# A two-block model on one core: second output product issued inside the last head's work, and the end done by tiles of 128 tokens

## The chip, the core and the metric

The kernel runs on one NeuronCore of a Trainium2 chip. The engines named below are PE (TensorE, matrix products; PEld is its weight load), DVE (VectorE), ACT (ScalarE), POOL (GpSimd) and SP (SyncE, which here only issues DMAs). The metric is the device time of one execution in microseconds (us); lower is better. All data are float32, and each float32 product shows as two MATMUL records in the trace (a transposition by the identity as one).

## The reference

Two blocks on 512 tokens of width 1024. The first is a mixer and an MLP. The second is a latent attention and a gated recurrence of 8 heads, merged and multiplied by `w_out`, then a mixture of 32 experts, of which each token takes 4, and a last norm. What matters here:

```python
# second block, after the attention y_mla has been computed
y_hg = hgrn2_readout(o_forward + flip(o_backward), gate, hg_norm_g)      # 8 heads of 128 features
y    = sigmoid(p7) * y_mla + sigmoid(p8) * y_hg                          # merged, head by head
x    = x + mod[2] * (y @ w_out)                                          # second output product
h    = rmsnorm(x, norm_ffn_g) * (1 + mod[4]) + mod[3]
logits = h @ w_router + b_router                                         # top 4 of 32, softmax
out  = sum over k of prob[token, k] * y_rows[dest[token, k]]             # weighted sum of 4 expert rows
x    = x + mod[5] * out
return rmsnorm(x, final_norm_g)
```

## The kernel before

Activations lie with features on the partitions: `x` is 8 chunks (`DC`) of 128 features by 512 tokens (`T`). `TT` is 4 tiles of 128 tokens. Each engine has its own program, in one fixed order, and they meet at semaphores. Dense weights arrive through a ring of 5 SBUF slots, loaded by SP when the products of an older tile are done.

**The heads of the recurrence** (loop over `n` from L1069). A head is a chain through DVE, ACT, POOL and PE: gates, two scans, key transpositions (L1086), state terms (L1093), 14 levels of small products of 128 by 64 (L1109), a diagonal (L1111, L1112), the output sum (L1119 to L1121), a norm (`norm`, L884; the root on ACT L1326; `norm_spread`, L894), and `merge` on DVE (L1755 to L1759), which completes features 128n to 128n+127 of `ymla` and signals `s_hg`. PE fills its waits in head n with the input products of head n+1 (`Filler`, L847). Its share per place comes from `HEAD_SLOTS`. The last head, n = 7, has no filler.

**After the last head**: `products("out2")`, 64 products of 128x512 (L847) from `ymla` and four weight tiles, in pairs of banks which ACT copies to `mout2` (L1319). Then DVE adds 8 chunks to `x` (L1832), squares them one by one for the norm (L1572) while PE sums them (L884), and with root and reciprocal done writes the router input `h3` by two instructions a chunk (L1714, L1715). PE's 32 router products (L1136) wait for all 8 chunks. Then come transposition (L1144), top 4, the table of blocks, and the experts.

**The experts**: 84 fixed blocks of 32 token rows (L1206 up, L1228 down), their 12 tiles of 1 MB per expert streamed by SP through 20 slots (18 in `space`, two in `x`, whose content was stored to `x_kept`). Then comes a loop for rows left over, which turns once here, with 12 loads more (L726).

**The end**: the result rows of the loop are stored by ACT (L1515). When that has landed, POOL issues 16 indirect gathers of 128 rows (L809), four for each token tile, into 8 buffers. DVE weighs and sums four rows for each tile (L1989, L1992). PE transposes the sum (L1291), ACT copies it (L1550), and DVE scales it and adds it to `x` (L1977, L1978), which SP has loaded back after the last expert product (L728). Only when all four tiles are added do the squares, root, `norm_spread` and the 8 last products (L1580) run, each chunk of 128 features by 512 tokens followed by its store (L731).

## Time and profile before

| | |
|---|---|
| device time, median of 3 runs | 3423.99 us (3416.69 to 3424.7) |
| the profiled execution: its own time, its span | 3431.33 us, 3429.3 us |
| PE busy (matmul) | 3031.8 us, 88% of the span |
| DVE, ACT, POOL busy | 982.5, 650.8, 189.7 us |
| mean granted TensorE clock | 0.919 of 2.4 GHz |
| HBM read | 551.58 MB |
| chain that ended last | PE 76%, DMA 10%, DVE 9%, ACT 2% |

### The profile page before, as it was taken

How to read it: one execution, taken by the hardware profiler on the slowest of the kernel's cores; microseconds unless marked ns; L12 is line 12 of the kernel's file. 1: busy time of each engine (PE TensorE's matmuls, PEld its weight loads, DVE VectorE, ACT ScalarE, POOL GpSimd, SP SyncE). 2: the span in 40 equal slices, each digit the busy share in tenths (PEclk: the TensorE clock that was granted, in tenths of full speed). 3: DMA queues.
4: the chain of work that ended last, by engine and by line, in shares of the span. 5: the costliest groups of instructions: out<-in, count | busy, mean ns of one | idle time of the engine just before them, and what ended most of it. 6: DMA issues, size and time to landing. Idle time of an engine off the chain costs nothing.

```text
span 3429.3 us, 45858 instructions
## 1 busy us (share of the span) xinstructions
PE 3031.8 (88%) x19729; PEld 1567.8 (46%) x19729; DVE 982.5 (29%) x1996; ACT 650.8 (19%) x1345; POOL 189.7 (6%) x180
## 2 busy tenths in 40 slices
PE   6899879999798999899989967689999999999993
PEld 3554434444344666666656655343333333333331
DVE  2243130000313221554444553322121112121224
ACT  1133000000001333444344332110101101111100
POOL 0000000000000000111111111020000000000002
PEclk9998889999898999999999976789999999998996
DMA  4134212211200112311111010198999979999695
GB/s 155 46 144 174 84 49 74 76 59 63 90 30 25 39 44 78 143 44 44 43 44 40 22 37 2 75 409 337 416 374 381 416 309 416 401 392 384 263 378 224
DMA packets 116909, 585.12 MB, mean 171 GB/s; under 512 B 10244, under 2 KB 21540, under 8 KB 69860
## 3 DMA queue, kind: packets, MB, share of 16 engines
q1 hardware_dynamic: 92752, 536.14, 39.4%
q10 hardware_dynamic: 17652, 24.25, 1.9%
q0 software_dynamic: 6304, 21.80, 1.8%
q8 instruction: 156, 2.56, 0.3%
q14 instruction: 45, 0.37, 0.0%
HBM read 551.58 MB, written 30.57 MB: 170 GB/s over the span
## 4 chain that ended last, share of the span: by engine, by line
PE 76%; DMA 10%; DVE 9%; ACT 2%; issue 1%; another core or an unknown queue 1%; ACTq 0%; SPq 0%; POOL 0%; DVEq 0%; POOLq 0%
PE product_banks L847 38%; PE product_banks L1206 13%; PE product_banks L1228 8%; DMA space<-in_wgu 7%; PE score_banks L1109 3%; DMA x<-in_wgu 2%; PE out_bank L974 1%; PE out_bank L894 1%; PE score_banks L911 1%; PE out_bank L933 1%; DVE sq L1572 1%; PE turn_bank L884 1%; PE product_banks L834 1%; PE score_banks L955 1%
## 5 line engine op out<-in xcount | busy, mean ns | idle before, releaser
L847 PE MATMUL product_banks<-space 128*128 128x512 f32 (+2 forms) x4016 | 1439.8, 511 | 36.1 <-DVE space L1793 13.4
L847 PEld LDWEIGHTS product_banks<-space 128*128 128x128 f32 x4016 | 711.7, 196 | 647.7 <-issue 583.1
L1206 PE MATMUL product_banks<-space 128*32 128x512 f32 x4848 | 582.4, 614 | 54.0 <-DMA space<-in_wgu 53.0
L1206 PEld LDWEIGHTS product_banks<-space 128*32 128x32 f32 x4848 | 141.2, 111 | 373.6 <-issue 268.4
L1228 PE MATMUL product_banks<-space,rstd 128*32 128x256 f32 x5024 | 302.0, 393 | 2.4 <-ACT rstd L1511 1.2
L1319 ACT ACTIVATE space<-product_banks 128x512 f32<-128x512 f32 (+1 forms) x234 | 114.4, 525 | 857.2 <-PE product_banks L847 836.1
L1926 DVE TENSOR_TENSOR sq<-product_banks,cst 128x512 f32<-128x512 f32 x85 | 58.8, 692 | 748.9 <-PE product_banks L1206 748.9
L1228 PEld LDWEIGHTS product_banks<-space,rstd 128*32 128x32 f32 x5024 | 168.4, 114 | 162.9 <-issue 73.2
L760 POOL TENSOR_TENSOR space<-space 128x512 f32<-128x512 f32 x112 | 131.6, 1189 | 1032.6 <-ACT space L1452 934.0
L1109 PE MATMUL score_banks<-space 128*128 128x64 f32 x896 | 134.3, 303 | 28.0 <-issue 21.1
L1109 PEld LDWEIGHTS score_banks<-space 128*128 128x128 f32 x896 | 131.2, 225 | 36.8 <-issue 32.5
L1572 DVE TENSOR_TENSOR sq<-space 128x512 f32<-128x512 f32 (+1 forms) x58 | 33.1, 606 | 375.6 <-PE turn_bank L884 237.9
L884 PE MATMUL turn_bank<-sq,cst 128*32 128x128 f32 (+1 forms) x784 | 49.1, 348 | 88.8 <-DVE sq L1572 88.7
L1507 ACT ACTIVATE ms<-sq 128x256 f32<-128x256 f32 x85 | 35.4, 417 | 455.3 <-DVE sq L1929 455.3
L1511 ACT ACTIVATE rstd<-turn_bank 128x256 f32<-128x256 f32 x85 | 32.6, 383 | 366.0 <-PE turn_bank L1217 366.0
L1206 PE MATMUL product_banks<-x,space 128*32 128x512 f32 x592 | 74.6, 618 | 4.9 <-DMA x<-in_wgu 4.9
L1814 DVE COPY_PREDICATED space<-cst,score_banks 128x256 f32<-128x256 uint8 x112 | 58.3, 521 | 67.2 <-PE score_banks L1109 66.5
L1699 DVE TENSOR_TENSOR space<-space 128x1024 f32<-128x1024 f32 x16 | 19.6, 1225 | 200.1 <-ACT space L1319 200.1
L1822 DVE TENSOR_TENSOR space<-space 128x256 f32<-128x256 f32 x112 | 71.4, 637 | 12.8 <-ACT space L1469 12.8
L884 PEld LDWEIGHTS turn_bank<-sq,cst 128*32 128x32 f32 x784 | 18.1, 126 | 124.0 <-DVE sq L1572 94.6
L782 POOL DMA_INDIRECT cst<-h_rows,space x21 | 19.9, 948 | 927.6 <-PE score_banks L1195 921.7
L1940 DVE TENSOR_TENSOR zeros<-product_banks,cst 128x256 f32<-128x256 f32 x84 | 35.7, 425 | 122.7 <-PE product_banks L1228 115.9
(291 smaller groups left out, 2400.2 us busy)
## 6 DMA issues: line engine op xcount, KB each, us to landing
space<-in_wgu SPq DMA_DIRECT2D x230, 1024.0 KB, 21.7
space<-in_wdn SPq DMA_DIRECT2D x116, 1024.0 KB, 21.1
space<-in_wt SPq DMA_DIRECT2D x104, 1024.0 KB, 5.4
x<-in_wgu SPq DMA_DIRECT2D x26, 1024.0 KB
y_rows<-zeros ACTq DMA_DIRECT2D x2, 6400.0 KB, 29.7
x<-in_wdn SPq DMA_DIRECT2D x12, 1024.0 KB
y_rows<-zeros ACTq DMA_DIRECT2D x84, 128.0 KB
space<-in_wt SPq DMA_DIRECT2D x13, 512.0 KB, 4.4
```

Of the source, the lines that this page charges most:

```text
L760: gp.tensor_tensor(dlt[:, L % 2, 0:T].rearrange("p (b s) -> p b s", s=2 * hf), c3, ref.broadcast_to([P, nb, 2 * hf]), ALU.subtract).then_i ...
L847: ins = nc.tensor.matmul(bank[0:rows, at:at + cols], lhsT, rhs, start=(i == 0), stop=(i == len(mm) - 1))
L884: ins = nc.tensor.matmul(PT[ROWS * q:ROWS * q + ROWS, 0:w // 4], ones[:, 0:ROWS], sq[:, g % 2, w // 4 * q:w // 4 * (q + 1)], start=(c == 0 ...
L1109: ins = nc.tensor.matmul(LB[L % 2][:, 64 * c:64 * c + 64], X[:, L % 2, cs_], half, start=True, stop=True)
L1206: ins = nc.tensor.matmul(bank[ROWS * g:ROWS * g + ROWS, :], xT_[:, k, :], w[:, 512 * g:512 * g + 512], start=(k == 0), stop=(k == DC - 1))
L1228: ins = nc.tensor.matmul(bank[ROWS * g:ROWS * g + ROWS, :], aT_[:, P * c + ROWS * d:P * c + ROWS * d + ROWS], w[:, c, 256 * g:256 * g + 25 ...
L1319: ins = nc.scalar.activation(dst, src, func, bias=bias, scale=scale)
L1572: V.tensor_tensor(sq[:, g % 2, 0:w], src[:, c, 0:w], src[:, c, 0:w], ALU.mult).then_inc(s_sq, 1)
L1814: V.copy_predicated(to, mk, LB[L % 2][:, 0:256].rearrange("p (c b s) -> p c b s", c=TT, s=hf)).then_inc(s_at, 1)
L1822: V.tensor_tensor(xv[:, :, qh], ev[:, :, qh], views(qq, hf)[:, :, qh], ALU.mult)
L1926: V.tensor_tensor(tbuf, bank, bias[:, 0:512], ALU.add).then_inc(s_u, 1)
L1940: V.tensor_tensor(to, bank, bias[:, 512:768], ALU.add).then_inc(s_y, 1)
```

## The change

1. **Second output product.** `mout2` and its pairs are gone. A `MixFiller` gives the last head 28 of the 64 products: features of heads 0 to 6, output chunks 0 to 3, summed in four product banks. After `merge` of head 7 come 4 products that complete these chunks, then output chunks 4 to 7, 8 products each. DVE adds each chunk to `x` out of the bank and squares it at once, and PE sums two chunks' squares after each block (`norm_sum`).
2. **Router input.** DVE writes `h3` by one instruction a chunk, ACT adds the shift, and PE's router products wait chunk by chunk.
3. **Loads at the end.** `x` is loaded back before the 12 loads of the last loop, for which `more_slot` uses slots of `space` alone.
4. **The end by tiles.** All 16 gathers have a buffer of their own. Of a tile's four rows ACT weighs the first, DVE adds the second, and PE adds the third and fourth to the transposed sum by products with diagonals of weights (`weigh`). Each tile gets its own addition to `x` (DVE), squares and gain (ACT), sum of squares (`sum_squares`, PE), root (ACT), reciprocal and last product (DVE, `finish`), and its own store of 128 tokens by 1024 features, in runs of 512 bytes.

```diff
@@ (SP)
-                sp.wait_ge(s_res, 2)
+                sp.wait_ge(s_o2x, DC)
                 sp.dma_start(xkept, x).then_inc(s_xkept, 16)
...
+                for i in range(NS_SPACE, NS):
+                    sp.wait_ge(*released[i + NS * (loads_of_slot[i] - 1)])
+                sp.dma_start(x, xkept).then_inc(s_xback, 16)
...
-                sp.wait_ge(s_dn, n_more + N_FIXED_BLOCKS)
-                sp.dma_start(x, xkept).then_inc(s_xback, 16)
-                for c in range(DC):
-                    sp.wait_ge(s_norm, normed("final", c + 1))
-                    sp.dma_start(out[:, c, :], fin[:, c, :]).then_inc(s_end, 16)
...
+                for i in range(TT):
+                    sp.wait_ge(s_fin, i + 1)
+                    sp.dma_start(out[:, :, P * i:P * i + P], fin[:, :, P * i:P * i + P]).then_inc(s_end, 16)
@@ (POOL)
-                    if j >= YBUF:
-                        gp.wait_ge(s_acc, j - YBUF + 1)
-                    gp.indirect_dma_start(yg[:, j % YBUF, :], None, yrows,
-                                          bass.IndirectOffsetOnAxis(desti_u[:, j:j + 1], 0)).then_inc(s_yg[j % YBUF], 16)
+                    if j >= 8:
+                        gp.wait_ge(*yg_landed(j - 8))
+                    gp.indirect_dma_start(yg[:, j, :], None, yrows,
+                                          bass.IndirectOffsetOnAxis(desti_u[:, j:j + 1], 0)).then_inc(s_yg[j % 8], 16)
@@ (PE)
+                def lead(self, n):
+                    for _ in range(n):
+                        k, c = divmod(self.done, 4)
+                        t = out2_tiles[c // 2]
+                        if k == 0 and c % 2 == 0:
+                            pe.wait_ge(s_slot[t % RING], 16 * (t // RING + 1))
+                        if c == 0:
+                            pe.wait_ge(s_hg, k + 1)
+                        nc.tensor.matmul(jb[c], out2_weight(c, k), ymla[:, k, :], start=(k == 0), stop=False)
+                        self.done += 1
+
+                def fill(self, i):
+                    self.lead(4 * (DC - 1) * sum(HEAD_SLOTS[:i + 1]) // sum(HEAD_SLOTS) - self.done)
...
-            products("out2")
+            for c in range(4):
+                nc.tensor.matmul(jb[c], out2_weight(c, DC - 1), ymla[:, DC - 1, :], start=False, stop=True).then_inc(s_o2, 1)
+            for t in out2_tiles[2:]:
+                pe.wait_ge(s_slot[t % RING], 16 * (t // RING + 1))
+            for c in range(4, DC):
+                pe.wait_ge(s_o2x, c - 3)
+                for k in range(DC):
+                    ins = nc.tensor.matmul(jb[c - 4], out2_weight(c, k), ymla[:, k, :], start=(k == 0), stop=(k == DC - 1))
+                ins.then_inc(s_o2, 1)
+                norm_sum("ffn2", 2 * c - 8)
+                norm_sum("ffn2", 2 * c - 7)
...
+            pe.wait_ge(s_weigh, 1)
             for i in range(TT):
-                pe.wait_ge(s_acc, TOPK * i + TOPK)
-                if i:
-                    pe.wait_ge(s_tTc, i)
+                bank = row_banks[i % 2]
+                pe.wait_ge(s_acc, i + 1)
+                if i >= 2:
+                    pe.wait_ge(s_xt, i - 1)
                 for c in range(DC):
-                    ins = nc.tensor.transpose(S[:, P * c:P * c + P], acc[:, i, P * c:P * c + P], ident)
-                ins.then_inc(s_tT, 1)
-            norm("final")
-            norm_spread("final")
+                    nc.tensor.matmul(bank[:, P * c:P * c + P], acc[:, i, P * c:P * c + P], ident, start=(c % 4 == 0), stop=False)
+                for k in (2, 3):
+                    j = TOPK * i + k
+                    pe.wait_ge(*yg_landed(j))
+                    for c in range(DC):
+                        ins = nc.tensor.matmul(bank[:, P * c:P * c + P], yg[:, j, P * c:P * c + P], weigh[:, 2 * i + k - 2, :], start=False, stop=(k == 3 and c % 4 == 3))
+                    if k == 2 and i:
+                        sum_squares(i - 1)
+                ins.then_inc(s_sum, 1)
+            sum_squares(TT - 1)
@@ (ACT)
+            for c in range(DC):
+                act.wait_ge(s_h3, c + 1)
+                nc.scalar.activation(h3[:, c, :], h3[:, c, :], F.Identity, bias=modv[:, 24 + c, 0:1]).then_inc(s_norm, 1)
...
+            weigh_first(0)
+            weigh_first(1)
             for i in range(TT):
-                act.wait_ge(s_tT, i + 1)
-                nc.scalar.activation(yT[:, :, P * i:P * i + P], v3(S[:, :], DC), F.Copy).then_inc(s_tTc, 1)
-            norm_root("final")
+                ts = slice(P * i, P * i + P)
+                act.wait_ge(s_xt, i + 1)
+                if i >= 2:
+                    act.wait_ge(s_fmm, i - 1)
+                nc.scalar.activation(v3(squares[:, i % 2, :], DC), x[:, :, ts], F.Square).then_inc(s_fsq, 1)
+                for c in range(DC):
+                    ins = nc.scalar.activation(fin[:, c, ts], x[:, c, ts], F.Copy, scale=vcol("final_norm_g_2", c))
+                ins.then_inc(s_gain, 1)
+                act.wait_ge(s_fmm, i + 1)
+                nc.scalar.activation(ms[:, ts], PT[:, 0:P], F.Sqrt, bias=const("eps"), scale=1.0 / D).then_inc(s_frt, 1)
+                if i + 2 < TT:
+                    weigh_first(i + 2)
@@ (DVE)
             for c in range(DC):
-                ins = V.scalar_tensor_tensor(x[:, c, :], mout2[:, c, :], modv[:, 16 + c, 0:1], x[:, c, :], ALU.mult, ALU.add)
+                g = chunk0[NI["ffn2"]] + c
+                dve.wait_ge(s_o2, c + 1)
+                V.scalar_tensor_tensor(x[:, c, :], jb[c % 4], modv[:, 16 + c, 0:1], x[:, c, :], ALU.mult, ALU.add).then_inc(s_o2x, 1)
+                dve.wait_ge(s_o2x, c + 1)
+                dve.wait_ge(s_mm, g - 1)
+                V.tensor_tensor(sq[:, g % 2, :], x[:, c, :], x[:, c, :], ALU.mult).then_inc(s_sq, 1)
...
+            add_second(0)
+            dve.wait_ge(s_xback, 16)
             for i in range(TT):
+                ts = slice(P * i, P * i + P)
+                if i + 1 < TT:
+                    add_second(i + 1)
+                dve.wait_ge(s_sum, i + 1)
+                for c in range(DC):
+                    ins = V.scalar_tensor_tensor(x[:, c, ts], row_banks[i % 2][:, P * c:P * c + P], modv[:, 40 + c, 0:1], x[:, c, ts], ALU.mult, ALU.add)
+                ins.then_inc(s_xt, 1)
+                if i:
+                    finish(i - 1)
+            finish(TT - 1)
```

The order of instructions on PE after the output sum of the last head (L1121 before), before the change. `turn_bank` holds the sums of squares, `out_bank` the spread roots, `product_banks` the product:

```order
L1121 MATMUL out_bank<-space 128x128
L884 MATMUL turn_bank<-sq,cst 32x128 x4
L894 MATMUL out_bank<-rstd,cst 128x128 x4
L847 MATMUL product_banks<-space 128x512 x64
L884 MATMUL turn_bank<-sq,cst 32x128 x32
L894 MATMUL out_bank<-rstd,cst 128x128 x4
L1136 MATMUL out_bank<-space 32x128 x32
```

And of the change, from its last level (L1149) and diagonal on, with rows left out where the same pair repeats:

```order
L1149 MATMUL score_banks<-space 128x64 x4
L911 MATMUL product_banks<-space 128x512
...
L911 MATMUL product_banks<-space 128x512 x2
L927 MATMUL turn_bank<-sq,cst 32x128 x4
L937 MATMUL out_bank<-rstd,cst 128x128 x4
L1168 MATMUL product_banks<-space 128x512 x4
L1174 MATMUL product_banks<-space 128x512 x8
L927 MATMUL turn_bank<-sq,cst 32x128 x8
```

Of the 64 products that stood after the spread, 36 stand there now (4 and four times 8). One product stands between most of the levels, 13 in all, two behind the output sum, and the other 13 stand ahead of the levels.

DVE at the end, before the change: rows of four token tiles (L1989, L1992), the additions to `x` (L1977, L1978), then the norm over all tokens:

```order
L1989 TENSOR_SCALAR space<-space 128x1024
L1992 SCALAR_TENSOR_TENSOR space<-space 128x1024 x3
L1977 TENSOR_TENSOR space<-space,mod 128x8x128
L1978 TENSOR_TENSOR x<-x,space 128x8x128
...
L1572 TENSOR_TENSOR sq<-x 128x512 x8
L1574 RECIPROCAL rstd<-ms 128x128
L1580 SCALAR_TENSOR_TENSOR space<-x,vec,out_bank 128x512 x8
```

And of the change: the weight diagonals (L2066), the second rows (L2073), additions to `x` out of the banks (L2090), and `finish` (L2078, L2080):

```order
L2066 TENSOR_SCALAR space<-cst,space 128x128 x8
L2073 SCALAR_TENSOR_TENSOR space<-space 128x1024 x2
L2090 SCALAR_TENSOR_TENSOR x<-score_banks,mod,x 128x128 x8
L2073 SCALAR_TENSOR_TENSOR space<-space 128x1024
L2090 SCALAR_TENSOR_TENSOR x<-product_banks,mod,x 128x128 x8
L2078 RECIPROCAL rstd<-ms 128x128
L2080 TENSOR_TENSOR space<-space,rstd 128x8x128
```

DVE's 16 instructions on gathered rows have become 4, and the norm stands tile by tile one tile behind the additions. The second row of tile i+2 stands ahead of the additions of tile i+1, and it waits for ACT's weighing of the first row.

PE at the end, of the change (before, it had the 32 transpositions of L1291, then the 32 and 4 instructions of the norm):

```order
L1351 MATMUL score_banks<-cst,space 128x128 x8
L1356 MATMUL score_banks<-space 128x128 x16
L1351 MATMUL product_banks<-cst,space 128x128 x8
L1356 MATMUL product_banks<-space 128x128 x8
L1341 MATMUL turn_bank<-space,cst 128x128 x8
L1356 MATMUL product_banks<-space 128x128 x8
```

Each tile now has 24 products of 128 by 128, and 8 for the squares of the tile before it stand between the third and the fourth row.

## Rows read from the trace of the kernel before

**Rows 1.** Busy time by stage: PE, PEld, DVE, ACT, POOL, granted clock, DMA share, GB/s.

```profile
2037.00:2117.00 80.00, 42.42 (x201) 39.27 (x201) 44.80 (x80) 23.79 (x46) 16.43 (x14) 0.54 0.00 1
2117.00:2175.00 58.00, 57.17 (x128) 24.90 (x128) 0.00 (x0) 4.05 (x8) 0.00 (x0) 0.96 0.01 3
3374.00:3406.00 32.00, 6.26 (x26) 5.09 (x27) 23.68 (x21) 3.07 (x3) 17.57 (x16) 0.50 0.73 262
```

**Rows 2.** The chain that ended last, from the end of head 7's merge to the transpositions.

```profile
2116.87 57.32 PE product_banks L847 x128
...
2182.37 0.70 PE turn_bank L884 x8
...
2189.52 2.09 PE out_bank L894 x8
2194.09 0.67 DVE space L1714
...
2204.86 1.82 PE score_banks L1144 x8
```

**Rows 3.** Timeline of PE in head 6, which has a filler.

```profile
1981.52 1.94 PE L1109 MATMUL score_banks<-space 128*128 128x64 f32 x8 [3.51 <-issue]
1988.04 1.00 PE L1109 MATMUL score_banks<-space 128*128 128x64 f32 x8
2016.98 0.39 PE L1120 MATMUL out_bank<-space 128*128 128x128 f32 x2
2017.21 0.39 PE L1121 MATMUL out_bank<-space 128*128 128x128 f32 x2
```

**Rows 4.** Windows of 5 us at the end of head 7 (columns as rows 1).

```profile
2097.00:2102.00 5.00, 5.00 (x24) 5.00 (x25) 2.54 (x6) 0.00 (x0) 0.00 (x0) 0.50 0.00 0
...
2117.00:2122.00 5.00, 5.00 (x7) 2.10 (x8) 0.00 (x0) 0.00 (x0) 0.00 (x0) 0.59 0.10 26
2122.00:2127.00 5.00, 5.00 (x13) 2.28 (x12) 0.00 (x0) 0.00 (x0) 0.00 (x0) 1.00 0.00 0
```

**Rows 5.** Timeline around the last expert loads and the result store.

```profile
3326.30 5.12 SPq L726 DMA_DIRECT2D space<-in_wgu  x6
...
3364.14 0.35 SPq L728 DMA_DIRECT2D x<-x_kept  x1
...
3364.83 1.08 ACTq L1515 DMA_DIRECT2D y_rows<-conditions  x1
3373.36 0.18 POOL L779 TENSOR_TENSOR space<-space 1x1 f32<-1x1 f32 x1 [108.77 <-DMA y_rows<-conditions]
```

**Rows 6.** Windows of 4 us around the last expert loads (columns as rows 1).

```profile
3316.00:3320.00 4.00, 4.00 (x42) 1.20 (x38) 0.00 (x0) 0.38 (x1) 0.00 (x0) 1.00 1.02 417
...
3324.00:3328.00 4.00, 4.00 (x52) 1.53 (x48) 0.55 (x2) 0.00 (x0) 0.00 (x0) 1.00 0.46 126
```

**Rows 7.** Timeline of the end, all engines.

```profile
3378.47 0.85 DVE L1989 TENSOR_SCALAR space<-space 128x1024 f32<-128x1024 f32 x1 [13.83 <-DMA space<-y_rows,space]
...
3386.80 4.06 DVE L1992 SCALAR_TENSOR_TENSOR space<-space 128x1024 f32<-128x1024 f32 x3 [0.52 <-DMA space<-y_rows,space]
3387.47 1.02 ACT L1550 ACTIVATE space<-score_banks 128x1024 f32<-128x1024 f32 x1 [28.70 <-PE score_banks L1291]
...
3408.67 1.28 ACT L1326 ACT_TABLE_LOAD   x1
...
3418.15 0.95 DVE L1574 RECIPROCAL rstd<-ms 128x128 f32<-128x128 f32 x1 [1.17 <-ACT ms L1326]
...
3421.27 5.36 DVE L1580 SCALAR_TENSOR_TENSOR space<-x,vec,out_bank 128x512 f32<-128x512 f32 x8 [2.17 <-PE out_bank L894]
```

**Rows 8.** Timeline: single instructions on tiles of 128 by 128.

```profile
2050.81 2.07 PE L1093 MATMUL turn_bank<-space 128*128 128x128 f32 x8 [0.90 <-ACT space L1455]
...
2072.17 1.11 DVE L1793 SCALAR_TENSOR_TENSOR space<-space,turn_bank 128x128 f32<-128x128 f32 x3
...
2204.92 0.37 ACT L1482 ACTIVATE space<-out_bank,space 128x128 f32<-128x128 f32 x1 [16.45 <-PE out_bank L1136]
```

149 lines of the change are left out of this document (86 added, 63 removed).

## The prediction, made before the run

> **What bounds the kernel now.** I read the stages first, then the chain that ended last, then the timeline at the two places of the change. Three stretches matter. (a) From head 7's merge to the router the chain runs almost wholly through one engine at a time: PE makes 64 products in 57.32 us while DVE is idle, then DVE works while PE is idle, until PE's router products end at 2204.86 [rows 1, 2]. The products start when the merge has ended, at 2116.87, so the stretch takes 88.0 us. (b) During the last head PE has no filler and is busy for 42.42 of 80 us [rows 1]. At its end PE is busy without a pause, at the 1.2 GHz level (granted 0.50), on 24 records in 5.00 us [rows 4]. (c) At the end DVE is the bound: 23.68 busy of 32 us while PE does 6.26 [rows 1], then the norm over all tokens, and 8 last products of 5.36 us, which start only at 3421.27 [rows 7]. The experts between (a) and (c) keep PE and DMA near full. Nothing in them is changed, so I take them as a block of fixed length, which starts earlier when the router does.
>
> **(a) Second output product.** Removed: 28 of 64 products. 57.32 / 64 = 0.90 us each. The first 5 us run at a granted 0.59 and the next at 1.00 [rows 4], so some 2.3 us of the 57.3 are the cold start and remain: (57.3 - 2.3) x 36/64 + 2.3 = 33.2 us. Six of eight sums of squares now stand between the blocks. At 0.70 each, cold and with its wait [rows 2], that would be 4.2; at the high clock a stream of these costs about half, and I take 2.7. DVE's additions and squares lie beside the blocks of 6.9 us. A square of chunk c waits for the sum of chunk c-2, so DVE does not run ahead, yet each block leaves it 6.9 us for 2 x 1.5. What remains behind the last block is one addition, one square and one sum: 0.76 + 0.70 + 0.70 = 2.2. Root and reciprocal stay: 1.8. The spread of 2.09 may find the clock still high: 1.6. Then 8 products on DVE, 0.67 each [rows 2], make 5.4, plus one ACT instruction (0.7) and one chunk of router products (0.5): 6.6, where before 2204.86 - 2191.61 = 13.2 stood. Sum: 33.2 + 2.7 + 2.2 + 1.8 + 1.6 + 6.6 = 48.1, against 88.0. **Gain 39.9 us**; bounds 37 (products at 0.90, sums at 0.70, spread 2.09) and 42.
>
> **(b) The last head.** Added to its PE stream: 28 products, 24 us at the high clock, 48 at the low. Three stand ahead of the spread of head 6, in a wait for ACT and DVE. Eight more lie in PE's waits for DVE's scans, where nearly all of its 38 us of idleness are [rows 1]; even at the low clock they are only 8 x 1.7 = 14. Two single ones stand between key transposition and state terms, where PE waits 0.90 us for ACT's copy [rows 8]: hidden at the high clock (0.86), +0.8 each at the low. 13 stand between the levels. There PE is the bound in both kernels. Before, a level costs 8 records x 5.00/24 = 1.67 us [rows 4]. With filler and high clock it costs 0.84 + 0.86 = 1.70. So the filler is free if it raises the clock. Head 6 says that it does: its levels begin at 1.94 for 8 records and are at 1.00 four levels later [rows 3], with filler of products of 128 columns; products of 512 keep PE no less busy. Cold start of the levels +2; diagonal behind them at the high clock 1.8 less; spread of head 7 1.0 less; one single product +0.8. Sum about 0; since the last transpositions and state terms may also run warm (1 less), I take **gain 1 us**, bounds -4 and +4.
>
> **(c) The end.** Three parts. *The load of x*: 2 MB at the 417 GB/s of full queues [rows 6] is 5 us, now ahead of the 12 last loads. But between 3324 and 3328 the queues move only 126 GB/s [rows 6], and `x` may be requested when the last product of the expert before the last is done, 1 us before the first of these loads at 3326.3 [rows 5]. So I take +4.1 us for the last tile and for the result behind it. In return the result store is alone: it was issued at 3364.83, 0.7 us behind the 2 MB of x, and landed at 3373.3, 8.5 us [rows 5]. Alone I take 3 us, bounds 2.5 and 8.5. Together -1.4, bounds -2 and +4.
>
> *The tiles.* The gathers keep their pace of 1.3 to 1.5 us (the first lands at 3378.47, the sixth at 3386.8 [rows 7]), and the 16th lands near 3400. A product of 128 by 128 costs 0.23 us at the high clock (2016.98 to 2017.21 [rows 3]) and 2.07/4 = 0.5 at the low, the last one's drain included [rows 8]; eight are 1.8 or 3.5. PE can start tile 0 when DVE has added the second row (it lands some 4 x 1.5 us before the sixth, at 3380.8, and takes 1.3), at 3382.1; it starts cold and rises as it did behind 2117 [rows 4]: bank ready at 3389.3. An addition to `x` of 128 by 128 out of a bank: 0.37 with its own wait [rows 8], 0.3 in a row; 8 are 2.4, so x of tile 0 is there at 3391.7. From there a ring of waits sets the pace: ACT squares (1.1), 8 gains, root (0.4), weighing of the first row two tiles on (1.1); DVE its second row (4.06/3 = 1.35 [rows 7]) and then the next tile's additions (2.4). A gain is 0.37 alone [rows 8], 0.3 in a row: 2.4. The ring is 8.7 us, PE's four parts of 1.8 (7.2) lie beside it. Tile 1: 3391.7 + 8.7 + 1.28 (table load) = 3401.7; tile 2: 3410.4. Tile 3 follows PE: second row at 3408.0, two parts to 3411.6, squares of tile 2 to 3413.4, last part 3415.2, additions 3417.6. Then square 1.1, gains 2.4, root 0.4, reciprocal 0.95, product 1.2: 3423.7, and the last store. Before, 3429.3 - (3421.27 + 5.36) = 2.7 us passed behind the last product [rows 7] for a store of 256 KB; now it has 512 KB in runs of 512 bytes, 3.1 to 5: 3427 to 3429 against 3429.3. **Gain of the tiles 1.5 us**, bounds -5 (additions at 0.37, gains at 0.37, slow store) and +5.
>
> The Trainium skill's ScalarE page (ScalarE: Activation LUTs, "What ACT_TABLE_LOAD costs") speaks against moving the gains to ACT: a pointer operand adds a fixed cost to every instruction, whatever its width, and only some 0.09 us overlap between neighbours. By it a gain is 0.29 us in a row, 2.4 for eight; by the row alone (0.37) it would be 3.0, and the end 2 us later. The row of 0.37 agrees with the page's single instruction.
>
> **The sum.** 39.9 + 1 + 1.4 + 1.5 = 43.8, say 44 us. Span 3429.3 - 44 = 3385; the profiled execution's own 3431.33 would become 3387. It lies 7.3 us above the median of the runs shown, whose own spread is 8. I take the difference off the median: 3424 - 44 = **3380 us**.
>
> **Rivals.**
> *Low clock at the end.* If PE's waits between tiles let the clock fall each time, every part costs 3.5 and not 1.8. Four parts (14 us) then exceed the ring. Tile 0's bank is there at 3392.4, x of tile 3 at 3435.5, the end near 3446, 18 us later than in my sum: 3398. For it: the clock is at 0.50 through the whole of the old end [rows 1]. Against it: PE would then be busy without a pause on 128 columns, which is just what raised it in head 6. The Trainium skill (TensorE: Matmul & The Clock Gate, "HAM oscillation") describes the same trap: work in bursts with waits between is throttled anew each time. Chance 0.14; a mixture between both is within my range.
> *Low clock in the last head.* Then each of 13 levels costs 1.67 + 1.71: +22 us, and 3402. For it: 5.00 of 5 us busy on the levels alone did not raise the clock [rows 4]. Chance 0.06.
> *Slower than before.* One mechanism: the clock stays low wherever the change puts new PE work, also in the 36 remaining products (1.71 each, +28). 22 + 18 + 28 = 68 against a gain of 44: 3448. It decides from 44 us on. Against it: the same products rose to 1.00 after 5 us [rows 4]. Chance 0.02.
> *The change does nothing.* The experts end when their 384 loads of 1 MB end. If these did not start with the router's table but were held by something else, (a) would be swallowed, and about 3421 remain. The first loads wait for that table in the code, so chance 0.02.
> *A better end.* If instructions in a row on DVE and ACT cost 0.25 and the store alone 2.5, the end is 5 to 9 us earlier: 3373. Chance 0.12.
> My own forecast, 3371 to 3391: 0.64.
>
> **Range and chances.** 3367 to 3397 takes in my case, the better end and half of the low clock at the end, also the scatter of some 4 us of a median. A measurement of this kernel tells about 0.3% (10 us) from no change. Faster by more than that: 0.96. Within: 0.02. Slower: 0.02.
>
> **What would show it.** Right: 36 products in 33 us behind head 7's merge, and 48 us from the merge to the router's last product; head 7 no longer than before, its levels at 1.7 us with the clock at 1.00 from the third or fourth on; the last expert tile 4 us later after the router, the result store 3 us; gathers with no waits; 9 us from tile to tile at the end; experts unchanged in length. Wrong: levels of 3.4 us; a granted 0.50 between 3385 and 3425; a gap on PE ahead of the blocks of output chunks 4 to 7 because DVE's square still waits; a last store of over 5 us; the stretch of the experts grown by more than 4 us, since its 84 fixed blocks meet the loads in another phase.

## The result and the profile after

The changed kernel takes 3378.77 us (median of 4 runs, 3373.34 to 3387.42) where the kernel before takes 3424.34: a ratio of 0.988, interval 0.9861 to 0.990. Timed once more, unaltered (e7), it came to 3382.3 against 3423.64, a ratio of 0.9878 (0.9861 to 0.9895). So the gain is 41 to 46 us, and 44 was forecast. The profiled execution is the longest of its four, 3387.42 us with a span of 3385.6 (43.7 less than the span before) at a mean granted clock of 0.937 (0.919 before).

First the stages, in windows of the changed kernel (columns as in [rows 1]). The first row answers to the last head of [rows 1], the second is the stretch of the remaining products, the third the spread ahead of the router, the fourth the 32 us from the first gather on.

```profile
2037.00:2117.00 80.00, 53.10 (x246) 37.56 (x247) 43.71 (x77) 23.80 (x46) 16.58 (x14) 0.78 0.01 2
2117.00:2152.00 35.00, 34.42 (x127) 14.74 (x125) 10.67 (x16) 0.00 (x0) 0.00 (x0) 0.96 0.00 0
2154.00:2158.00 4.00, 2.07 (x8) 1.78 (x8) 1.83 (x4) 0.57 (x1) 0.00 (x0) 0.52 0.86 365
3329.00:3361.00 32.00, 21.21 (x152) 21.05 (x153) 10.17 (x21) 11.77 (x23) 15.75 (x16) 0.74 0.72 269
```

In the last head TensorE is now busy 53.10 of 80 us at 0.78 of the full clock, not 42.42 at 0.54. Behind the merge DVE's 16 additions and squares (10.67 us) lie beside the products instead of after them. At the end work has gone from DVE (10.17 us, 23.68 before) to TensorE (21.21 us, 6.26 before).

The chain that ended last, from the merge to the router's last product, the answer to [rows 2]:

```profile
2115.19 6.09 PE product_banks L1168 x8
2121.28 6.87 PE product_banks L1174 x16
2128.15 0.57 PE turn_bank L927 x16
...
2144.00 7.08 PE product_banks L1174 x16
...
2151.11 0.76 DVE x L1924
...
2154.53 2.09 PE out_bank L937 x8
...
2163.47 1.49 PE score_banks L1193 x8
```

The merge ends at 2115.19, the router's products at 2163.47: 48.3 us, where 88.0 stood. There is no pause between the blocks of products; the sums of squares between them cost 0.57 a pair, and TensorE waits for nothing of DVE's there.

TensorE's timeline in head 7, the answer to [rows 3, 4]: L1149 are the level's 8 records, L911 the filler's product.

```profile
2072.43 1.94 PE L1149 MATMUL score_banks<-space 128*128 128x64 f32 x8 [2.63 <-DVE space L1884]
2074.16 2.02 PE L911 MATMUL product_banks<-space 128*128 128x512 f32 x2
...
2083.52 1.00 PE L1149 MATMUL score_banks<-space 128*128 128x64 f32 x8
2084.35 1.08 PE L911 MATMUL product_banks<-space 128*128 128x512 f32 x2
2085.27 1.00 PE L1149 MATMUL score_banks<-space 128*128 128x64 f32 x8
```

The first levels run at the lower clock (1.94 for 8 records); from 2083.5 on a level and its product begin every 1.75 us.

The loads and the result's store, the answer to [rows 5]:

```profile
3280.10 0.35 SPq L734 DMA_DIRECT2D x<-x_kept  x1
3281.79 6.08 SPq L747 DMA_DIRECT2D space<-in_wgu  x8
...
3324.96 1.08 ACTq L1583 DMA_DIRECT2D y_rows<-conditions  x1
3328.49 0.18 POOL L798 TENSOR_TENSOR space<-space 1x1 f32<-1x1 f32 x1 [108.92 <-DMA y_rows<-conditions]
```

Counted in the chain, from issue to landing, the store takes 3.4 us instead of 8.4. And the timeline of the tiles, the answer to [rows 7]:

```profile
3333.69 1.15 ACT L1620 ACTIVATE space<-space 128x1024 f32<-128x1024 f32 x1 [17.02 <-DMA space<-y_rows,space]
3337.25 3.75 PE L1351 MATMUL score_banks<-cst,space 128*128 128x128 f32 x16 [13.04 <-DVE space L2073]
3345.16 2.16 DVE L2090 SCALAR_TENSOR_TENSOR x<-score_banks,mod,x 128x128 f32<-128x128 f32 x8 [1.41 <-PE score_banks L1356]
...
3354.83 3.05 PE L1351 MATMUL score_banks<-cst,space 128*128 128x128 f32 x16 [2.54 <-DVE space L2073]
3357.67 2.62 PE L1356 MATMUL score_banks<-space 128*128 128x128 f32 x16
3360.13 1.95 PE L1341 MATMUL turn_bank<-space,cst 128*128 128x128 f32 x16
3362.12 0.37 ACT L1635 ACTIVATE ms<-turn_bank,cst 128x128 f32<-128x128 f32 x1 [1.85 <-PE turn_bank L1341]
3362.38 1.14 ACT L1620 ACTIVATE space<-space 128x1024 f32<-128x1024 f32 x1
3363.56 1.28 DVE L2073 SCALAR_TENSOR_TENSOR space<-space 128x1024 f32<-128x1024 f32 x1 [4.59 <-ACT space L1620]
3364.76 2.15 DVE L2090 SCALAR_TENSOR_TENSOR x<-score_banks,mod,x 128x128 f32<-128x128 f32 x8
...
3375.64 3.36 PE L1341 MATMUL turn_bank<-space,cst 128*128 128x128 f32 x16 [3.34 <-ACT space L1630]
3380.43 1.23 DVE L2080 TENSOR_TENSOR space<-space,rstd 128x1024 f32<-128x1024 f32 x1
```

Read it from the bottom of the middle piece: DVE's second row of tile 3 (3363.56) waits 4.59 us for ACT's first (3362.38), which stands behind ACT's root of tile 1 (3362.12), which waits for a sum of squares (3360.13) that TensorE takes only behind the third rows of tile 2. TensorE itself had stood idle for 2.54 us before tile 2 and ran its first two parts slowly, in 3.05 and 2.62 us (granted 0.66 from 3355 to 3360). From the first gather to the end it takes 56.4 us, where the kernel before takes 55.2.

### The profile page after: what moved, and what is told of

The parts are those of the page before. It is cut to its first block, busy times and chain, and to the rows that moved or that the text cites. A ratio compares the mean times of both kernels' runs of the same rounds, so it can differ in the third digit from the quotient of the medians.

```text
span 3385.6 us, 46199 instructions
## 1 busy us (share of the span) xinstructions
PE 3034.3 (90%) x19881; PEld 1575.7 (47%) x19881; DVE 963.6 (28%) x1999; ACT 667.4 (20%) x1384; POOL 189.1 (6%) x180
## 4 chain that ended last, share of the span: by engine, by line
PE 77%; DMA 10%; DVE 8%; ACT 2%; issue 1%; SPq 1%; ACTq 0%; POOL 0%; DVEq 0%; POOLq 0%
PE product_banks L866 37%; PE product_banks L1255 13%; PE product_banks L1277 8%; DMA space<-in_wgu 6%; PE score_banks L1149 3%; DMA x<-in_wgu 2%; PE out_bank L1017 1%; PE out_bank L937 1%; PE score_banks L954 1%; PE out_bank L976 1%; SPq L729 1%; PE product_banks L1174 1%; PE turn_bank L927 1%; DMA space<-in_wdn 1%; DVE sq L1658 1%
## 5 line engine op out<-in xcount | busy, mean ns | idle before, releaser
L866 PE MATMUL product_banks<-space 128*128 128x512 f32 (+2 forms) x3888 | 1384.3, 508 | 32.3 <-DVE space L1884 13.4
L866 PEld LDWEIGHTS product_banks<-space 128*128 128x128 f32 x3888 | 687.3, 196 | 613.3 <-issue 552.7
L1149 PE MATMUL score_banks<-space 128*128 128x64 f32 x896 | 126.2, 289 | 27.3 <-issue 21.1
L1149 PEld LDWEIGHTS score_banks<-space 128*128 128x128 f32 x896 | 124.7, 212 | 42.1 <-issue 38.3
L927 PE MATMUL turn_bank<-sq,cst 128*32 128x128 f32 (+1 forms) x720 | 42.0, 329 | 74.4 <-DVE sq L1658 73.0
L1534 ACT ACTIVATE space<-space 128x256 f32<-128x256 f32 x112 | 47.3, 422 | 119.7 <-DVE space L1914 119.6
```

The costliest lines, as they stand in the source:

```text
L866: ins = nc.tensor.matmul(bank[0:rows, at:at + cols], lhsT, rhs, start=(i == 0), stop=(i == len(mm) - 1))
L927: ins = nc.tensor.matmul(PT[ROWS * q:ROWS * q + ROWS, 0:w // 4], ones[:, 0:ROWS], sq[:, g % 2, w // 4 * q:w // 4 * (q + 1)], start=(c == 0 ...
L1149: ins = nc.tensor.matmul(LB[L % 2][:, 64 * c:64 * c + 64], X[:, L % 2, cs_], half, start=True, stop=True)
L1534: nc.scalar.activation(ev[:, :, qh], dv[:, :, qh], F.Exp)
```

## The experiments

Executions that share all code differ by several us, and most of that arises ahead of the change: ACT copies the attention output of head 6 between 2008 and 2020 us after the start, in kernels that are the same up to there. So I read four stretches from each profile, which leave this scatter out: from that copy of head 6 to that of head 7; from there to ACT's bias on the router's scores; from there to the first gather; and from there to the end. They are differences of starts in each timeline (for the kernel before: 2019.64, 2107.73, 2204.92, 3374.11, end 3429.3). They have a scatter of their own. Head 7 takes 87.1 to 88.2 us whatever the kernel, and the stretch of the experts up to 3.7 us more or less in the same code (e1 and the kernel before).

| kernel | median (kernel before) | ratio, 95% | head 7 | to router | to 1st gather | to end | gap |
|---|---|---|---|---|---|---|---|
| before | 3424.34 | | 88.1 | 97.2 | 1169.2 | 55.2 | no |
| the change | 3378.77 (3424.34) | 0.988 (0.9861-0.990) | 88.2 | 56.8 | 1165.7 | 56.4 | no |
| e1 | 3380.56 (3422.12) | 0.987 (0.9856-0.9885) | 87.1 | 56.7 | 1165.5 | 55.4 | no |
| e2 | 3426.48 (3422.12) | 1.0012 (1.0002-1.0023) | 87.2 | 97.3 | 1162.6 | 61.5 | yes |
| e3 | 3406.29 (3422.12) | 0.9958 (0.9943-0.9972) | 87.2 | 81.3 | 1165.1 | 54.3 | no |
| e4 | 3382.67 (3422.12) | 0.988 (0.9865-0.9894) | 87.7 | 56.7 | 1165.5 | 58.5 | yes |
| e5 | 3380.86 (3423.64) | 0.9874 (0.9857-0.9892) | 88.2 | 56.8 | 1166.2 | 56.5 | no |
| e6 | 3381.35 (3423.64) | 0.9883 (0.9867-0.990) | 87.7 | 56.7 | 1165.4 | 53.7 | no |
| e7 | 3382.3 (3423.64) | 0.9878 (0.9861-0.9895) | 87.7 | 56.7 | 1165.4 | 56.5 | no |
| e8 | 3374.97 (3421.93) | 0.9857 (0.984-0.9873) | 88.2 | 55.6 | 1166.3 | 52.2 | yes |
| e9 | 3377.97 (3421.93) | 0.9872 (0.9856-0.9889) | 87.1 | 55.5 | 1163.1 | 56.1 | yes |
| e10 | 3387.59 (3422.04) | 0.9899 (0.9881-0.9917) | 87.7 | 55.6 | 1166.4 | 61.6 | no |
| e11 | 3372.22 (3422.04) | 0.9858 (0.9841-0.9875) | 87.7 | 55.6 | 1166.7 | 47.7 | no |
| e12 | 3372.53 (3422.64) | 0.9859 (0.9843-0.9876) | 87.7 | 55.6 | 1166.2 | 46.4 | no |

The last column says whether the profile holds a gap, a halt of TensorE of several us, that e2 and e4 first showed and that is described there. e7 is the change once more, e11 is e8 and e12 is e9 once more.

**e1, the middle alone.** The filler, the sums from the banks and the router's input are those of the change; the load of x, the slots of the last expert, gathers, tiles, norm and store those of the kernel before. Against the changed kernel, cut to a few lines:

```diff
-        NORMS += [("ffn2", x, 8, T)]
+        NORMS += [("ffn2", x, 8, T), ("final", x, 8, T)]
...
-                for i in range(NS_SPACE, NS):
-                    sp.wait_ge(*released[i + NS * (loads_of_slot[i] - 1)])
-                sp.dma_start(x, xkept).then_inc(s_xback, 16)
...
+            norm("final")
+            norm_spread("final")
```

> Only the part of the change between head 6 and the router: the filler of head 7, the six sums and squares taken straight from the banks, the router input a chunk at a time on DVE and ACT. The end is that of the kernel before. Theory (the parts add up, the end gave next to nothing): the profiled run loses 41.4 us up to the router's products, as the changed kernel did, and nothing after them, so 3383 in the median and 41.4 us in the span. Rival (the shorter middle collides with something later, a load or the clock of the stages behind the router, and the new end makes up for it): less than 36 us, 3389 or more. Rival (the new end costs more than it gives, so the middle alone does better than the whole change): under 3378.

Measured: 3380.56 us, 41.6 below the kernel before; 56.7 us to the router. The middle alone gives all that the whole change gives, as far as these intervals tell (ratio 0.987, and 0.988 for the change). The span is 50.8 us shorter than in the profile before, but 5.8 of that arose ahead of head 7 and 3.7 in the experts' stretch, which holds the same code in both.

**e2, the end alone.**

The other half: up to the router all is as in the kernel before. Against the changed kernel:

```diff
-                filler = Filler(f"hg{n + 1}", HEAD_SLOTS) if n < 7 else MixFiller()
+                filler = Filler(f"hg{n + 1}", HEAD_SLOTS) if n < 7 else None
...
+            products("out2")
...
+            norm("ffn2")
             norm_spread("ffn2")
```

> Only the end of the change: x is loaded ahead of the last expert's weights, the result rows are stored without that load beside them, the weighted sum, the norm and the store go by tiles of 128 tokens. The middle is that of the kernel before. Theory (from the whole change's trace: last tile of weights 1.5 us later, the result's store 5.0 us shorter, the tiles 1.2 us longer): 2.3 us faster, 3422. Rival (the tiles alone are a clear gain and the rest of the change hides it): 6 us or more faster, under 3419. Rival (the end costs time): above 3425.

Measured over 12 runs: 4.4 us slower, ratio 1.0012, the interval just clear of 1. The rival of a costly end holds, by its time. Its profile shows a thing that the changed kernel's did not:

```profile
3377.75 1.95 PE L1319 MATMUL product_banks<-cst,space 128*128 128x128 f32 x16
3379.53 0.83 PE L1324 MATMUL product_banks<-space 128*128 128x128 f32 x6
3381.11 0.27 PE L1324 MATMUL product_banks<-space 128*128 128x128 f32 x1 [0.74 <-issue]
3381.82 0.48 PE L1324 MATMUL product_banks<-space 128*128 128x128 f32 x2 [0.45 <-issue]
...
3383.94 0.84 PE L1324 MATMUL product_banks<-space 128*128 128x128 f32 x6 [1.13 <-issue]
3384.00 2.16 DVE L2049 SCALAR_TENSOR_TENSOR x<-score_banks,mod,x 128x128 f32<-128x128 f32 x8 [7.84 <-remote]
```

TensorE drops out of a row of 16 records that has no wait inside it, and DVE starts its additions 6.1 us after the product that fills tile 0's bank ends by the profile (3377.9, a modelled end). Both go on at 3384, in a stretch in which the gathers keep the DMA queues at 102%. I call this the gap. DVE is not held by itself: what it waits for is TensorE's signal, which the trace has at 3383.97, 0.03 us before DVE starts. In e4, e8 and e9 too this signal comes 0.02 to 0.03 us before DVE's start, 6.4, 6.1 and 3.7 us behind the product's end; in the change it comes 0.02 us behind it.

**e3, no filler in head 7.**

```diff
-                    self.lead(4 * (DC - 1) * sum(HEAD_SLOTS[:i + 1]) // sum(HEAD_SLOTS) - self.done)
+                    pass
...
-                        filler.lead(3)
+                        if n < 7:
+                            filler.lead(3)
...
             for c in range(4):
-                nc.tensor.matmul(jb[c], out2_weight(c, DC - 1), ymla[:, DC - 1, :], start=False, stop=True).then_inc(s_o2, 1)
+                for k in range(DC):
+                    ins = nc.tensor.matmul(jb[c], out2_weight(c, k), ymla[:, k, :], start=(k == 0), stop=(k == DC - 1))
+                ins.then_inc(s_o2, 1)
```

> The changed kernel with nothing of the second output product inside head 7: the 28 products that the filler ran there stand behind the merge with the other 36. Sums, squares and the end as in the change. Theory (the filler is free, head 7 lasts the same with and without it): 28 products of 0.883 us, or 24.7 us more, less 1 to 2 us that head 7's merge comes earlier by without them: 3401 to 3404. Rival (the filler is worth more than its products, since it keeps the clock up in head 7): merge of head 7 up to 1.7 us later than with it, 3405 to 3406. Rival (the filler delays head 7 by queueing ahead of products that the chain waits for): merge 4 us or more earlier, 3399 or less.

Measured: 3406.29. Its chain behind the merge:

```profile
2104.35 30.01 PE product_banks L1172 x64
2134.37 6.87 PE product_banks L1179 x16
```

The first four chunks take 30.01 us where the change has 6.09, 23.9 more for 28 products, or 0.85 each. Head 7 lasts 87.2 us without filler and 87.1 to 88.2 with it. So the filler is free, and worth its own products and 0.6 us more: the head's own spread, ahead of the merge, takes 1.99 us without it and 1.17 with it. It takes 81.3 against 56.8 us to the router. That the head would end 1 to 2 us earlier without the filler, as the theory had it, did not come; the median of 3406.29 lies by the rival in which the filler gives more than its products (3405 to 3406). Without it head 7 runs at a mean granted clock of 0.59 with TensorE busy for 48.1 us, with it at 0.83 and busy for 61.7 of the same 87 to 88 us: the higher clock makes room for the filler.

**e4, the weighing ahead.**

```diff
             weigh_first(1)
+            weigh_first(2)
...
                 ins.then_inc(s_gain, 1)
+                if i == 0:
+                    weigh_first(3)
                 act.wait_ge(s_fmm, i + 1)
...
-                if i + 2 < TT:
-                    weigh_first(i + 2)
```

> The changed kernel with ACT's first weighing of tile 2 moved ahead of tile 0's squares, and that of tile 3 ahead of tile 0's root. In the changed kernel each of them stands behind the root of the tile two before, which waits for a sum of squares that TensorE takes only behind the next tile's rows; DVE and TensorE stand idle for it at 3352 and 3362. Theory (this ring of waits sets the tiles' pace): tile 2 starts on TensorE about 2.5 us earlier, tile 3 about 4.5, and the end comes 4 to 5 us earlier, 3374 to 3375. Rival (the gathers' landing sets the pace, the last of them came at about 3353): tile 2 and 3 start no more than 1 us earlier, 3378. Rival (ACT waiting for tile 2's row holds up tile 0's squares and all behind them): slower, 3380 or more.

Measured: 3382.67, no gain, and the gap again, DVE's first addition at 3346.57, 6.4 us behind its bank (3340.2). From that addition to the end it takes 36.2 us and in the change 40.4, 4.2 less, which is what was expected of the opened ring. But the gap itself shortens what follows, since rows land meanwhile: e8 and e11, one program, take 29.9 us from this addition to the end with the gap and 31.7 without. So 4.2 is an upper figure for this edit. A clean one comes with e11.

**e5, x loaded late.**

```diff
-                sp.dma_start(x, xkept).then_inc(s_xback, 16)
                 if BLOCKS_AT[-1] == 1:
...
+                sp.wait_ge(s_dn, n_more + N_FIXED_BLOCKS)
+                sp.dma_start(x, xkept).then_inc(s_xback, 16)
                 for i in range(TT):
```

> The changed kernel with x loaded as in the kernel before, behind the last down product and beside the store of the last expert's rows; the slots of the last loads and the tiles are those of the change. What the trace shows of the two halves of this trade: the store of the result rows takes 3.4 us alone and 8.4 us beside the load of x, and from the router's bias to the first gather the changed kernel took 1165.7 us against 1169.2 before. Theory (the load in front costs little, since the tiles are awaited anyway and x comes while DMA has room): store back to 8.4 us, router to first gather 1169 us or more, 3 to 5 us slower than the change, 3382 to 3384. Rival (x ahead of the last loads delays the last tile by its own 4.1 us, and the two halves cancel): within 1 us of the change, 3378 to 3380. Rival (x in front costs more than the store gains): 3377 or less.

```profile
3319.18 0.34 SPq L748 DMA_DIRECT2D x<-x_kept  x1
...
3319.87 1.08 ACTq L1584 DMA_DIRECT2D y_rows<-conditions  x1
3328.60 0.18 POOL L799 TENSOR_TENSOR space<-space 1x1 f32<-1x1 f32 x1 [109.67 <-DMA y_rows<-conditions]
```

The store takes 8.6 us again, 5.2 more, yet from router to first gather it is 1166.2 us, against 1165.1 to 1166.7, 1165.9 in the mean, in nine of the ten profiles with both the new middle and x in front (e9 has 1163.1). The two halves show apart as well. The store of the last rows is issued 1156.8 us behind the router's bias in e5 and 1156.2 in e1, which loads x late too, but 1160.8 to 1162.4 us, 1161.6 in the mean, in those nine profiles. So x in front costs the last tile some 4.8 us and gives 5.2 back. The two halves cancel, as the rival had it. These are single profiles of a stretch that scatters (the kernel before has 1159.9, also with x late), so neither half is firm to better than some 3 us; that they cancel rests on the nine profiles, on e5's stretch and on its median, 3380.86 beside 3382.3 of e7.

**e6, gathers paced by use.** On top of e4:

```diff
                     if j >= 8:
                         gp.wait_ge(*yg_landed(j - 8))
+                    if j == 8:
+                        gp.wait_ge(s_acc, 2)
+                    if j == 12:
+                        gp.wait_ge(s_xt, 1)
```

> The kernel with ACT's weighing ahead (e4), with the gathers of tile 2 held until the rows of tile 1 are weighed, and those of tile 3 until tile 0 is added to x. In e4 and in the kernel with the end alone, TensorE stood in the middle of tile 1's products and DVE before its first addition for 6.1 and 6.3 us, though what they wait for had come, while the gathers kept the DMA queues 100% busy; they went on when the gathers ran out. Theory (the stall comes of the saturated DMA queues): no such gap, first gather to end 52 us instead of 58.5, and 5 us or more faster than e4, 3374 to 3377. Rival (it has another cause and comes at random): the gap of 6 us is there again, 3380 or more. Rival (the held gathers land late): tiles 2 and 3 wait for DMA, first gather to end 54 to 57 us.

Measured: no gap, but tile 3's first row lands so late (ACT weighs it at 3348.81, 25.3 us behind the first gather) that the roots behind it on ACT wait; 53.7 us to the end, 3381.35, where the theory had 5 us less than e4. The rival of rows that land late holds in part; one profile without a gap proves nothing yet.

**e7, the change once more**, without any edit.

> The changed kernel once more, unaltered. Its first profile did not show the gap of 6 us that two kernels with the same end showed. Theory (the gap depends on how gathers and engines fall together, and comes in part of the executions of each kernel): the time spreads over 3373 to 3387 as before, median 3379, and this profile may show it, in which case first gather to end is 62 instead of 56.4 us. Rival (the gap belongs to the two other kernels, e4's by its order on ACT): no gap, 56.4 us again. In both cases the middle (attention output of head 7 to the router's bias) takes 56.7 us.

No gap, 56.5 us to the end: the tiles' stretch repeats to 0.1 us, tile 2's slow parts (3.00 and 2.67 us) included.

**e8, ring opened and router's clock held.** On top of e4:

```diff
-                    if k == 2 and i:
-                        sum_squares(i - 1)
                 ins.then_inc(s_sum, 1)
+                if i:
+                    sum_squares(i - 1)
...
+            def idle_products(bank, n):
+                for _ in range(n):
+                    nc.tensor.matmul(bank[:, 0:P], ones, ident, start=True, stop=True)
...
+                if c == DC - 1:
+                    idle_products(jb[0], 4)
                 norm_sum("ffn2", 2 * c - 7)
...
+            idle_products(jb[0], 6)
             norm_spread("ffn2")
+            idle_products(jb[0], 7)
```

> The kernel with ACT's weighing ahead (e4), and besides: TensorE takes the sum of squares of a tile behind all rows of the next instead of between them, and idle 128x128 products (4, 6 and 7 of them, their results unused) stand on TensorE around the last sum of squares and the spread before the router. They fill a stretch of 3 us in which the granted clock fell from 1.00 to 0.50 in the changed kernel, ahead of a spread of 2.09 us and of router products at 0.65 us a chunk. Theory for the router (the low clock is the cost): spread about 1.1 us, attention output of head 7 to the router's bias 55 us instead of 56.7. Rival (the clock falls all the same, or DVE's input chunks of 0.67 us set the pace anyway): 56.0 or more. Theory for the end (the ring of waits on ACT's roots set the tiles' pace): first gather to end 49 to 50 us instead of 56.4, if the gap of 6 us does not come; with both, 3370 to 3373. Rival (the gathers set the pace): 54 us or more without a gap. If the gap comes in every execution of a kernel with the weighing ahead, as its two medians above the change's suggest: 55 to 56 us, 3377.

The window of e8 that answers to the third row of windows above, and its spread:

```profile
2154.00:2158.00 4.00, 4.00 (x34) 3.68 (x33) 2.47 (x4) 0.98 (x3) 0.00 (x0) 1.00 1.08 459
```

```profile
2155.28 1.16 PE L941 MATMUL out_bank<-rstd,cst 128*128 128x128 f32 x8
```

Granted 1.00 instead of 0.52, spread 1.16 instead of 2.07, and 55.6 us to the router instead of 56.7 (55.5 or 55.6 in all five profiles that have the idle products): the low clock there cost 1.1 us, the rest of the router's input is paced by DVE's 0.67 a chunk. The profile holds the gap, and still reaches the end in 52.2 us.

**e9, TensorE kept busy before tile 0.** On top of e8:

```diff
             pe.wait_ge(s_weigh, 1)
+            idle_products(DN[0], 20)
+            pe.wait_ge(*yg_landed(0))
+            idle_products(DN[0], 8)
```

> The kernel before this one in the list (e8), with 20 idle 128x128 products on TensorE once the last expert's rows are out and 8 more once the first gathered row is in, so that TensorE does not stand idle before tile 0. In the changed kernel tile 0 ran at a granted clock of 0.50: 3.75 and 4.3 us for what later tiles did in 1.95 and 3.9. Theory (the low clock costs tile 0 about 2.5 us and all behind it follows): first gather to end 2 to 3 us shorter than in e8. Rival (tile 1's rows land too late for a faster tile 0 to matter): within 1 us of e8. Rival (the idle products hold up tile 0): 1 us or more longer.

Tile 0's transposing products take 2.05 us instead of 3.75, then comes the gap, earlier and longer than elsewhere. ACT seems to be in it, with a wait of 5.3 us that the profile gives no releaser for. Below it stands the same instruction of e12, the same program without the gap:

```profile
3335.69 1.15 ACT L1631 ACTIVATE space<-space 128x1024 f32<-128x1024 f32 x1 [5.31 <-issue]
```

```profile
3343.33 1.15 ACT L1631 ACTIVATE space<-space 128x1024 f32<-128x1024 f32 x1 [4.49 <-DMA space<-y_rows,space]
```

It weighs tile 2's first row, 18.0 us behind the first gather in e9 and 17.3 in e12, where it waits for that row to land. So ACT waits for its row in both, in e9 at most 0.7 us longer; that ACT was held is not shown.

56.1 us to the end: this profile cannot price the clock.

**e10, two gathers in flight, and e11, e8 once more.** The edit of e10 on e8:

```diff
-                    if j >= 8:
-                        gp.wait_ge(*yg_landed(j - 8))
+                    if j >= 2:
+                        gp.wait_ge(*yg_landed(j - 2))
```

> The kernel with the ring of waits opened and the router's clock held (e8), with each gather held until the one two before it has landed, so that at most two are on their way and the DMA queues are not full. Theory (the gap of 5 to 10 us on TensorE and DVE, seen in four of the nine profiles of the new end and always while the gathers kept the queues at 100% or more, comes of full queues): no gap, DMA share under 1.0 through the gathers, first gather to end 47 to 49 us against e8's 52.2, and 3 to 5 us less in the median than e8 in the same call. Rival (the gap has another cause): it appears here too, between 12 and 23 us behind the first gather. Rival (rows now land too late): tiles wait for DMA and first gather to end is 52 us or more without a gap.

> The kernel e8 once more, unaltered, beside the one with two gathers in flight. If the gap belongs to a kernel, its profile shows it again between 17 and 23 us behind the first gather, and first gather to end is 52.2 us; if it comes at random, this profile may be free of it, with 46 us. The head to router's bias stretch takes 55.6 us again in both cases.

In e10 there is no gap, but every row is late: ACT weighs tile 1's first row 15.1 us behind the first gather instead of 11.5, and it takes 61.6 us to the end, 3387.59. From 3324 to 3364 the queues are busy for 65% and move 191 GB/s. Holding gathers back costs far more than the gap. In e11, the same program as e8, the gap is absent, and the chain of its end is TensorE's own:

```profile
3334.79 1.79 PE product_banks L1359 x16
3336.58 3.57 PE product_banks L1364 x32
3340.15 1.79 PE turn_bank L1349 x16
...
3350.87 3.59 PE product_banks L1364 x32
3354.46 0.02 issue
3354.48 2.17 DVE x L2099 x8
```

A tile every 7.15 us, with nothing between: 47.7 us to the end, 8.7 less than the change, all of it behind DVE's first addition (31.7 against 40.4 us). So the gap comes in one execution of a program and not in another. That also tells what it costs in e8's profile, 52.2 against 47.7 us.

**e12, e9 once more.**

> The kernel e9 once more (e8 with 28 idle 128x128 products before tile 0), since its profile held the gap, and held it earlier than the others: from 12.7 to 23.1 us behind the first gather, where e4, e2 and e8 had it from 17.5 to 22.3. Its tile 0 did start at the high clock (transposing products 2.05 us instead of 3.76). Theory (the gap is random, the high clock is a gain): either a profile without gap, with first gather to end 45 to 46 us against the 47.7 of e8's second profile, or the median within 1 us of e8's two (3375.0 and 3372.2) or below. Rival (a faster TensorE at the start meets the gathers and brings the gap about or lengthens it): the gap again, first gather to end 54 us or more, median 3376 or more.

No gap, 46.4 us to the end against e9's 56.1, 3372.53 in the median: the low clock at tile 0 costs 1.3 us of the 2 to 3 expected, for tile 1 now waits for its rows: DVE adds its second one at 3339.07, and TensorE stands idle for 0.72 us until that is done. The opened ring (3374.97 and 3372.22) and e12 (3372.53) are the fastest here, 47 to 50 us below the kernel before; e9, the same program as e12, has 3377.97. Three ratios of 0.9857 to 0.9859 lie 0.002, or some 7 us, below the change's, though the intervals still overlap at their edges.

## Why the prediction was right, and where it was not

The forecast was 3380, the sum 44 us, and its weight lay in (a).

**(a), 39.9 forecast, 39.7 measured** (88.0 to 48.3), and 40.4 to 40.6 from head 7's copy to the router, where the middle is that of the change. Term by term: products with six sums 33.2 + 2.7 = 35.9, measured 2151.08 - 2115.19 = 35.9; last addition, square and sum 2.2, measured 2.0; root and reciprocal 1.8, measured 1.4; router input 6.6, measured 2163.47 - 2156.65 = 6.8. That the first pair agrees to 0.1 is luck: the products took 34.2 against 33.2, the three pairs of sums 1.7 against 2.7. The other miss is the spread: 1.6 taken, 2.1 found, since the clock had fallen (granted 0.52); e8 shows what holding it gives, 1.1 us with all that follows.

**(b), 1 forecast, 0 measured.** e3 settles it: head 7 lasts the same with and without 28 products in it, its levels at 1.75 us against 1.70 forecast. The rival of a low clock in the last head is out.

**(c), the load of x: 1.4 forecast, nothing measured.** The store gained 5.2 in e5 (5.5 forecast), the load in front costs 4.8 (4.1 forecast); the sum of the two was a difference of near equals. The profiled pair shows 3.5 us less from router to gather (1169.2 to 1165.7), which looks like a gain of the change; e1 has it too (1165.5) with the old loads, so it isn't. So it is luck as well that the span fell by 43.7, just the 44 of the forecast: 3.5 of it are scatter, and 1.1 more lie ahead of head 6's copy. Without them the profiled pair gives 39.1.

**(c), the tiles: the step that failed.** Forecast was a gain of 1.5, measured a loss of 1.2 without the gap; from the first row landed to the end 49.5 us were forecast and 51.9 measured. The step that failed is "the ring is 8.7 us, PE's four parts of 1.8 (7.2) lie beside it". They are not beside it. ACT's weighing for the tile two on stands behind a root, the root waits for a sum of squares on TensorE, and that sum stands behind the third rows of the next tile, so three of TensorE's parts are a link of the ring. At 1.8 each they end about when ACT is free for the root anyway, so the sum would have come out, but they did not all take 1.8. Measured, DVE's additions begin at 3345.16, 3354.69, 3364.76 and 3372.35: the round with the table load takes 9.5 us (8.7 + 1.28 forecast), the next one 10.1 (8.7 forecast), the last 7.6 (7.2 forecast). In the round of 10.1 TensorE had idled for 2.5 us and took 3.05 and 2.62 for its first two parts, and ACT's root waited 1.85 us for the sum. e3 has the same end and kept its clock there; TensorE had idled for 1.63 us before tile 2, not 2.54:

```profile
3367.99 2.15 DVE L2095 SCALAR_TENSOR_TENSOR x<-product_banks,mod,x 128x128 f32<-128x128 f32 x8
3368.13 2.05 PE L1356 MATMUL score_banks<-cst,space 128*128 128x128 f32 x16 [1.63 <-DVE space L2078]
...
3373.79 0.37 ACT L1640 ACTIVATE ms<-turn_bank,cst 128x128 f32<-128x128 f32 x1 [0.21 <-PE turn_bank L1346]
...
3376.43 2.15 DVE L2095 SCALAR_TENSOR_TENSOR x<-score_banks,mod,x 128x128 f32<-128x128 f32 x8
```

There the root waits 0.21 us and the round takes 8.4, less than the 8.7 forecast. The last sum of squares shows the same: 3.36 us at the lower clock in the change, past ACT's gains, which the forecast had as cover, and 2.05 in e3. From DVE's first addition to the end e3 takes 37.5 us and the change 40.4, so the low clock is worth 2.9 us here. (e5 and e7, with the same end, have the low clock at both places as the change has.) e11 opens the ring and puts each sum behind all rows of the next tile; then TensorE has no waits, becomes the bound at 7.15 a tile, and the same stretch takes 31.7.

The price of a gain (ACT's scaling of one chunk) was right: 2.43 us for eight, 0.30 each. The Trainium skill (ScalarE: Activation LUTs, "What ACT_TABLE_LOAD costs") gives 0.29 in a row by its overlap of 0.09. The trace agrees.

The rival of a low clock at the end came true in small: 1.3 us at tile 0 (e12), about 1.4 at the last sum, tile 2's parts at 3.05 and 2.62 instead of 2.05 and 1.95, not the 18 us of every part. The Trainium skill's trap of bursts with waits between (TensorE: Matmul & The Clock Gate, "HAM oscillation") is what these rows show at a small scale; in e11, where the ring is opened, no part behind tile 0 is slow.

**What nothing forecast: the gap.** It stands in 4 of 12 profiles of the new end (4 of the 10 whose gathers are not held back) and in neither of the two of the old. e3 has it in miniature: TensorE halts once for 0.45 us, and its signal for tile 0 comes 0.6 us late. It costs 4.5 us in e8 (against e11) and 9.7 in e9 (against e12), and may be what makes e2 slower than the kernel before; whether it stood in the other executions cannot be seen. Its cause stays open. For full DMA queues: it comes only while the gathers run at 100% or more, and the two kernels that held them back had none. Against: six profiles with queues as full had none, but for e3's halt. Late loading of instructions does not explain it: between the first halt and the end of the gap the traces of e2, e4 and e9 have no packet on the queues of kind instruction, and e8 has one, as e11 has at the same place without a gap. DVE's wait is TensorE's late signal and ACT's wait is for a row, so TensorE alone is shown to halt.

One thing parts the profiles with the gap from the others, and it bears on whether the gap is the kernel's at all. Each of the 16 gathers leaves 16 records of its landing in the kept trace, 256 in all. The change, e5, e6, e7, e11 and e12 have all 256 and e10 has 254; e2 and e4 have 159, e8 has 156, e9 94, and e3 168 (of the old end, 236 and 255). The missing ones fall between some 10 and 22 us behind the first gather, where the gap stands (17 to 23), and in e9, whose gap begins at 12.7, from the first landings on. So where TensorE halts, records of the profiler are lost too. Either the recording has a part in the halt, or one crowding does both; e3, with 168 and a halt of only 0.45 us, shows that lost records alone do not make a long gap. No run tells these apart, and that the gap costs time in an execution that is not profiled is not shown.

## What to carry to other kernels

When work is cut in tiles so that engines overlap, write down for each engine the order of its instructions and follow one tile's chain through all of them: a ring of waits is as long as all of its links, and a short instruction placed behind a wait for another tile (here ACT's first weighing behind a root) makes the other engine a link. If that engine is TensorE, price its link at both clocks, for the ring's own waits can let the clock fall (8.4 us a round in e3, 10.1 in the change). Put what needs no result of this tile ahead of what waits for one. The filler in the last head was free because it lay in waits or raised the clock enough to make room for itself; measure such a filler by taking it out and looking at the stretch, not at the median. Where executions scatter ahead of the change (here by up to 11.5 us), compare stretches of the trace from a common anchor: the two short ones of the change and of e7 repeat to 0.1 us (56.8 and 56.7, 56.4 and 56.5). Measure a stretch's own scatter first: that of the experts is up to 3.7 us.
